# Rotary key in two products per k tile, and the residual gates' sums as split products placed inside the output projection

## The reference, cut to what matters

```python
h  = modulate(rmsnorm(x), sh1, sc1)        # 512 x 1024
hc = modulate(rmsnorm(ctx), csh1, csc1)    # 256 x 1024
p, pc = h @ w_in, hc @ w_in[:, :KR_END]    # columns: kv latent 256 | rotary key 32 | q latent 384 | conv | gates
k_rope = concat(pc[:, 256:288], rope2d(p[:, 256:288], ang))   # one 32 wide key for all 8 heads
q = rmsnorm(q latent) @ w_uq;  k_nope, v = rmsnorm(kv latent) @ w_ukv
o = softmax((q_nope k_nope' + q_rope k_rope') * scale) v
y = sigmoid(g_attn) * (o @ w_attn_out) + sigmoid(g_conv) * (conv branch @ w_conv_out)
x = x + g1 * (y @ w_o)                     # g1, g2: 1024 wide rows, from silu(c) @ w_ada + b_ada
x = x + g2 * conv_ffn(modulate(rmsnorm(x), sh2, sc2))
return rmsnorm(x) * final_g
```

## Time and profile before

| | |
|---|---|
| runs of the kernel | 827.55, 827.59, 828.06 us, median 827.59 |
| the profiled execution | 827.32 us, its span 825.3 us (2.0 us lie around the span) |
| mean granted TensorE clock | 0.994 of full |
| busy, share of the span | PE 98%, weight loads 81%, DVE 62%, ACT 45%, POOL 45% |
| matmuls | 3937 |
| moved by DMA | 97.8 MB, 119 GB/s |

### The profile page before, as it was taken

The page is one execution under the profiler, slowest core; times in us unless marked ns, Lnnn a source line. Parts: engine busy times, 40 slices in busy tenths (PEclk is TensorE's granted clock), DMA queues, the critical chain, the costliest instruction groups (busy, mean ns, idle before and its releaser), DMA issues.

```text
span 825.3 us, 11436 instructions
## 1 busy us (share of the span) xinstructions
PE 805.4 (98%) x3937; PEld 671.3 (81%) x3937; DVE 511.8 (62%) x649; ACT 371.9 (45%) x592; POOL 368.6 (45%) x193
## 2 busy tenths in 40 slices
PE   4999999999999999999999999999999999999997
PEld 3778888888888888888788988888888888888885
DVE  5877589688888388777205575455555556535535
ACT  7656575566666323223225654443344433221223
POOL 5325593535543445554534064444444442544430
PEclk9899999999999999999999999999999999999999
DMA  9742251111110887786263043332333321332212
GB/s 309 252 141 61 69 125 30 50 30 48 36 42 28 262 275 253 224 241 198 98 234 90 13 126 104 102 101 85 93 102 102 101 86 68 102 124 91 93 51 102
DMA packets 120289, 97.82 MB, mean 119 GB/s; under 512 B 13660, under 2 KB 106105, under 8 KB 120249
## 3 DMA queue, kind: packets, MB, share of 16 engines
q1 hardware_dynamic: 120137, 97.26, 38.5%
q10 hardware_dynamic: 112, 0.04, 0.0%
HBM read 95.17 MB, written 2.10 MB: 118 GB/s over the span
## 4 chain that ended last, share of the span: by engine, by line
PE 95%; DVE 2%; ACT 2%; DMA 1%; issue 0%; SPq 0%; DVEq 0%; ACTq 0%
PE ps L428 26%; PE ps L430 26%; PE ps L429 26%; PE ps L1762 8%; PE ps L1871 3%; PE ps L1860 2%; PE ps L1617 1%; DMA xt<-x_dram 1%; ACT work L749 1%; PE ps L1964 0%; PE ps L1908 0%; PE ps L1657 0%; PE ps L1916 0%; ACT parts L791 0%; DVE vs L1280 0%
## 5 line engine op out<-in xcount | busy, mean ns | idle before, releaser
L345 POOL TENSOR_TENSOR wlo<-raw,whi 128x1024 fp32r<-128x1024 f32 (+4 forms) x125 | 280.0, 2249 | 354.6 <-ACT whi L337 354.5
L428 PE MATMUL ps<-hhi,whi 128*128 128x512 f32 (+1 forms) x520 | 196.0, 377 | 0.2 <-DVE hlo L1476 0.2
L430 PE MATMUL ps<-hhi,wlo 128*128 128x512 f32 (+1 forms) x520 | 195.7, 376 | 0.0
L429 PE MATMUL ps<-hlo,whi 128*128 128x512 f32 (+1 forms) x520 | 195.5, 376 | 0.0
L337 ACT ACTIVATE whi<-raw 128x1024 fp32r<-128x1024 f32 (+4 forms) x125 | 118.3, 957 | 138.9 <-PE ps L430 48.8
L428 PEld LDWEIGHTS ps<-hhi,whi 128*128 128x128 f32 x520 | 97.8, 188 | 18.3 <-DVE hlo L1476 0.4
L430 PEld LDWEIGHTS ps<-hhi,wlo 128*128 128x128 f32 x520 | 97.8, 188 | 18.0
L429 PEld LDWEIGHTS ps<-hlo,whi 128*128 128x128 f32 x520 | 97.9, 188 | 17.7
L1502 DVE TENSOR_TENSOR raw<-raw,gbc 128x1024 f32<-128x1024 f32 x22 | 50.4, 2295 | 43.9 <-DMA raw<-w_down_dram 43.9
L1510 DVE SCALAR_TENSOR_TENSOR work<-ps,prm,work 128x511 f32<-128x511 f32 x44 | 33.0, 749 | 71.2 <-ACT work L1051 70.3
L1406 DVE SCALAR_TENSOR_TENSOR adacc<-ada,cvec,adacc 128x1024 f32<-128x1024 f32 x28 | 63.8, 2318 | 14.9 <-DMA ada<-w_ada_dram 14.9
(11 more groups left out here) (288 smaller groups left out, 1509.5 us busy)
## 6 DMA issues: line engine op xcount, KB each, us to landing
raw<-w_up_dram SPq DMA_DIRECT2D x88, 256.0 KB, 3.1
ada<-w_ada_dram SPq DMA_DIRECT2D x32, 512.0 KB, 6.1
raw<-w_in_dram SPq DMA_DIRECT2D x56, 256.0 KB, 4.4
raw<-w_down_dram SPq DMA_DIRECT2D x44, 256.0 KB, 2.8
adaraw<-w_ada_dram SPq DMA_DIRECT2D x32, 256.0 KB, 5.4
raw<-w_o_dram SPq DMA_DIRECT2D x16, 256.0 KB, 3.1
xt<-x_dram SPq DMA_DIRECT2D x4, 512.0 KB, 7.5
raw<-w_attn_out_dram SPq DMA_DIRECT2D x8, 256.0 KB, 2.9
```

What stands on the lines that cost most here:

```text
L345: ins = (engine or nc.gpsimd).tensor_tensor(out=l, in0=r, in1=h.bitcast(F32), op=ALU.subtract)
L428: pe.matmul(o, l[0], r[0], start=start, stop=False)
L429: pe.matmul(o, l[0], r[1], start=False, stop=False)
L430: return pe.matmul(o, l[1], r[0], start=False, stop=stop)
```

## The change

**The rotary key.** `key_hi` writes only the 64 key columns (32 plain, 32 swapped) of each k tile into the upper half of `whi` and then copies them, already rounded, into the upper half of `wlo`; `key_lo` zeroes the lower half of `whi` and puts the low parts into the lower half of `wlo`. `key_pair` makes two matmuls per k tile: `wlo` x hi, which gives lo x hi in rows 0 to 63 and hi x hi in rows 64 to 127, and `whi` x lo, which adds hi x lo in rows 64 to 127. The two halves have to be added: ACT copies rows 0 to 63 of banks 3 and 0 to partitions 64 to 127, behind a wait for `w_used` of `U_KR + 1`, before the squares of the kv latent; DVE adds. The key's operations for the latent tokens (`rotary_key`, four of them) move behind the reciprocals of head 1; the context's addition stays ahead of head 0. The first rotary product, which stood ahead of the sum of squares, goes.

**The gates.** ACT and DVE split the two rows into `hhi` and `hlo` (no longer read by then) in the last turn of the merge; ACT also writes ones as fp32r. `gate_rows` makes 2 x 4 fp32r matmuls into banks 4 to 7. The output projection starts with t = 0, 1 of k = 0 to 3 (48 matmuls), then the gates' sums, then t = 0, 1 of k = 4, then t = 2, 3 of k = 0 to 4, which now count `w_used`. SP's wait ahead of the residual load is for the DVE's splits and `cols2_ps` instead of the gates' sums.

```diff
-            if isinstance(u, int) and U_KR <= u < U_KR + 2:
-                return headed_raw(slot, DT // 2), headed(whi, slot, DT // 2), headed(wlo, slot, DT // 2)
...
+        def key_tiles(t, slot):
+
+            return t[:, slot, 0:DT // 2 * P].rearrange("p (k n) -> p k n", n=P)
+
+        def key_parts(v, at):
+
+            r = v[:, :, at + ROPE:at + 2 * ROPE].rearrange("p g (a h j) -> p g a h j", a=2, h=2)
+            return [v[:, :, at:at + ROPE], r[:, :, :, 0, :], r[:, :, :, 1, :]]
+
+        def key_hi(act, u, slot):
+
+            arrived(act, u, slot)
+            wait(act, w_used, u - SLOTS + 1)
+            for r, h in zip(headed_raw(slot, DT // 2), key_parts(key_tiles(whi, slot), NOPE)):
+                if h.shape[-1] == ROPE:
+                    r = r[:, :, NOPE:QK]
+                ins = nc.scalar.activation(h, r, ACT.Copy)
+            ins.then_inc(w_hi, 1)
+            act.wait_ge(w_hi, u + 1)
+            nc.scalar.activation(key_tiles(wlo, slot)[:, :, NOPE:P], key_tiles(whi, slot)[:, :, NOPE:P], ACT.Copy).then_inc(s("kr_hi"), 1)
+
+        def key_lo(pool, u, slot):
+
+            wait(pool, w_used, u - SLOTS + 1)
+            nc.gpsimd.memset(key_tiles(whi, slot)[:, :, 0:NOPE].bitcast(F32), 0.0).then_inc(s("chl_zero"), 1)
+            pool.wait_ge(w_hi, u + 1)
+            pool.wait_ge(s("chl_zero"), u - U_KR + 2)
+            for r, h, l in zip(headed_raw(slot, DT // 2), key_parts(key_tiles(whi, slot), NOPE), key_parts(key_tiles(wlo, slot), 0)):
+                if h.shape[-1] == ROPE:
+                    r = r[:, :, NOPE:QK]
+                ins = nc.gpsimd.tensor_tensor(out=l, in0=r, in1=h.bitcast(F32), op=ALU.subtract)
+            ins.then_inc(w_lo, 1)
+
...
+        kr_ctx = cx0[:, 0:C]
...
+        gate_hi, gate_lo = hhi[:, 0:4, :], hlo[:, 0:4, :]
+        ones_r = hhi[:, 4, 0:P]
+
+        def gate_value(n):
+
+            return adacc[:, 3 * n * D:(3 * n + 1) * D].rearrange("p (a n) -> p a n", n=512)
...
                 if k == 6:
-                    sp.wait_ge(s("gbc_ps"), 4)
+                    sp.wait_ge(s("ada2_used"), 4 * DT + 2)
+                    sp.wait_ge(s("cols2_ps"), 1)
...
-            for u in range(U_KR, U_UQ[2]):
+            for u in range(U_KR, U_KR + 2):
+                key_lo(pool, u, u % SLOTS)
+            for u in range(U_KR + 2, U_UQ[2]):
...
             for u in (U_KR, U_KR + 1):
-                split_hi(act, u, u % SLOTS)
+                key_hi(act, u, u % SLOTS)
...
             for u in (*U_UQ[0:2], U_CX0):
                 split_hi(act, u, u % SLOTS)
+            used(act, U_KR + 1)
+            nc.scalar.activation(krot2[NOPE:P, :], ps[0:NOPE, 3, :], ACT.Copy).then_inc(s("kr_hi"), 1)
+            nc.scalar.activation(kr_ctx[NOPE:P, :], ps[0:NOPE, 0, 0:C], ACT.Copy).then_inc(s("kr_hi"), 1)
             for m in range(KVT):
                 act.wait_ge(s("lat_ps"), QT + KVT + m + 1)
...
                     else:
+                        if d == DT - 1:
+                            act.wait_ge(s("ada2_used"), 4 * DT)
+                            for g in range(2):
+                                nc.scalar.activation(gate_hi[:, 2 * g:2 * g + 2, :], gate_value(g), ACT.Copy).then_inc(s("g_sig"), 1)
+                            nc.scalar.activation(ones_r, ones[:], ACT.Copy).then_inc(s("g_sig"), 1)
                         act.wait_ge(s("m_sum"), d + 1)
                         nc.scalar.activation(mhi[:, d, :], work[:, w + 2, :], ACT.Copy).then_inc(s("m_hi"), 1)
...
-            dve.wait_ge(s("kr_ps"), 1)
-            dve.wait_ge(s("tab_loaded"), 16)
-            kr, tmp = krot[NOPE:QK, :], krot2[NOPE:QK, :]
-            kr_ps, kr_ctx = ps[:, 3, :], ps[:, 0, 0:C]
-            nc.vector.tensor_tensor(out=kr_ps[NOPE:QK, :], in0=kr_ps[NOPE:QK, :], in1=tab[NOPE:QK, :], op=ALU.mult).then_inc(s("kr"), 1)
             dve.wait_ge(s("p_sq"), QT + 2)
             nc.vector.tensor_tensor(out=sqk[0], in0=sqk[0], in1=sqk[1], op=ALU.add).then_inc(s("k_ssq"), 1)
+            kr, low = krot[NOPE:QK, :], krot2[NOPE:P, :]
+            dve.wait_ge(s("q_sum"), QT - 1)
             used(dve, U_KR + 1)
-            nc.vector.tensor_tensor(out=tmp, in0=kr_ps[QK:P, :], in1=tab[QK:P, :], op=ALU.mult).then_inc(s("kr"), 1)
-            nc.vector.tensor_copy(kr[:, T:K], kr_ctx[NOPE:QK, :]).then_inc(s("kr"), 1)
-            dve.wait_ge(s("kr"), 3)
-            nc.vector.tensor_tensor(out=kr[:, 0:T], in0=kr_ps[NOPE:QK, :], in1=tmp, op=ALU.add).then_inc(s("kr"), 1)
+            dve.wait_ge(s("kr_hi"), 4)
+            nc.vector.tensor_tensor(out=kr[:, T:K], in0=ps[NOPE:QK, 0, 0:C], in1=kr_ctx[NOPE:QK, :], op=ALU.add).then_inc(s("kr"), 1)
+
+            def rotary_key():
+
+                dve.wait_ge(s("tab_loaded"), 16)
+                nc.vector.tensor_tensor(out=ps[NOPE:P, 3, :], in0=ps[NOPE:P, 3, :], in1=low, op=ALU.add).then_inc(s("kr"), 1)
+                dve.wait_ge(s("kr"), 2)
+                nc.vector.tensor_tensor(out=krot2[QK:P, :], in0=ps[QK:P, 3, :], in1=tab[QK:P, :], op=ALU.mult).then_inc(s("kr"), 1)
+                nc.vector.tensor_tensor(out=ps[NOPE:QK, 3, :], in0=ps[NOPE:QK, 3, :], in1=tab[NOPE:QK, :], op=ALU.mult).then_inc(s("kr"), 1)
+                dve.wait_ge(s("kr"), 4)
+                nc.vector.tensor_tensor(out=kr[:, 0:T], in0=ps[NOPE:QK, 3, :], in1=krot2[QK:P, :], op=ALU.add).then_inc(s("kr"), 1)
...
                     dve.wait_ge(s("k_rms"), 1)
                     nc.vector.reciprocal(k_inv, k_rms).then_inc(s("k_rinv"), 1)
+                    rotary_key()
...
-                    nc.vector.tensor_tensor(out=g, in0=ps[:, n, :], in1=g, op=ALU.add).then_inc(s("gbc_sum"), 1)
+                    nc.vector.tensor_tensor(out=g, in0=ps[:, 4 + n, :], in1=g, op=ALU.add).then_inc(s("gbc_sum"), 1)
...
                 if d == DT - 1:
+                    for g in range(2):
+                        dve.wait_ge(s("g_sig"), 2 * DT + g + 1)
+                        nc.vector.tensor_tensor(out=gate_lo[:, 2 * g:2 * g + 2, :], in0=gate_value(g),
+                                                in1=gate_hi[:, 2 * g:2 * g + 2, :].bitcast(F32), op=ALU.subtract).then_inc(s("ada2_used"), 1)
                     norm2_mods()
...
+            def key_pair(o, slot, k, hi, lo):
+
+                at = slice(k % 4 * P, (k % 4 + 1) * P)
+                pe.matmul(o, wlo[:, slot, at], hi[:, k, :], start=k == 0, stop=False)
+                return pe.matmul(o, whi[:, slot, at], lo[:, k, :], start=False, stop=k == DT - 1)
+
             pe.wait_ge(s("mods1"), 2 * DT)
             for n in range(2):
                 u = U_KR + n
                 unit(u)
-                last = project(pe, ps[:, 3, :], u % SLOTS, hhi[:, 4 * n:4 * n + 4, :], hlo[:, 4 * n:4 * n + 4, :], kt=DT // 2,
-                               start=n == 0, stop=n == 1)
-            last.then_inc(s("kr_ps"), 1)
+                pe.wait_ge(s("kr_hi"), n + 1)
+                for k in range(4 * n, 4 * n + 4):
+                    key_pair(ps[:, 3, :], u % SLOTS, k, hhi, hlo)
...
-                last = mm3(pe, ps[:, 0, 0:C], (tile_of(whi, u % SLOTS, k % 4), tile_of(wlo, u % SLOTS, k % 4)),
-                           (chi[:, k, :], clo[:, k, :]), k == 0, k == DT - 1)
+                last = key_pair(ps[:, 0, 0:C], u % SLOTS, k, chi, clo)
...
                 if h == 2:
-                    pe.wait_ge(s("kr"), 3)
+                    pe.wait_ge(s("kr"), 1)
...
-                pe.wait_ge(s("m_prod"), 2 * DT - 2)
-                for n, at in enumerate((0, 512, 3 * D, 3 * D + 512)):
-                    pe.matmul(ps[:, n, :], ones[:], adacc[:, at:at + 512], start=True, stop=True).then_inc(s("gbc_ps"), 1)
+                pe.wait_ge(s("m_prod"), 2 * DT)
+                pe.wait_ge(s("mods2"), 1)
+                pe.wait_ge(s("g_sig"), 2 * DT + 3)
+                pe.wait_ge(s("ada2_used"), 4 * DT + 2)
+                for n in range(4):
+                    pe.matmul(ps[:, 4 + n, :], ones_r, gate_hi[:, n, :], start=True, stop=False)
+                    pe.matmul(ps[:, 4 + n, :], ones_r, gate_lo[:, n, :], start=False, stop=True).then_inc(s("gbc_ps"), 1)
...
-            gate_rows()
...
+            pe.wait_ge(s("m_prod"), 2 * DT - 2)
             for k in range(5):
+                if k == 4:
+                    gate_rows()
                 unit(U_O + k)
                 pe.wait_ge(s("m_lo"), k + 1)
-                for t in (2, 3, 0, 1):
-                    if k == 0 and t == 2:
-                        pe.wait_ge(s("mods2"), 1)
-                        pe.wait_ge(s("m_prod"), 2 * DT)
-                    if k == 0 and t < 2:
-                        pe.wait_ge(s("gbc_sum"), 2 * t + 2)
+                for t in range(2):
+                    for n in range(2):
+                        out_rows(k, t, n)
+            for k in range(5):
+                for t in range(2, TT):
+                    if k == 0:
+                        pe.wait_ge(s("gbc_sum"), 2 * t - 2)
                     for n in range(2):
```

(23 more changed lines are left out.)

## The result

The changed kernel takes 830.05 us (median of 7 runs, 829.74 to 831.83), the kernel before 827.59 in the same comparison: ratio 1.0034, 95% interval 1.0024 to 1.0044, so 2.5 us slower. The forecast was 826.5 and a range that ended at 828.5. The profiled execution took 829.74 us, its span is 827.8 and its mean granted clock 0.995; for the kernel before these were 827.32, 825.3 and 0.994. So the mean clock of this one execution shows nothing of what follows. The other six runs of the changed kernel have 0.991 four times (829.83 to 830.32 us) and 0.987 twice (831.54 and 831.83 us), while 58 of the 59 runs of the kernel before that were taken beside the experiments have 0.992 or more.

A forecast was written before the change was run, and what follows sets the result against it. TensorE was taken as the bound, with 95% of the chain of waits. 827.32 + 0.51 - 1.57 = 826.26 us, plus 0.27 for the median of the runs, gave 826.5 us; range 825.4 to 828.5.

The forecast's parts named there:

- Part A: Rotary key: 2.76 us of matmuls removed from TensorE, all spent in waits; 0.51 us later at the first sum of squares.
- two waits: TensorE waits for DVE's first `cqlo` before the context, then for ACT's kv latent copies before the first sum of squares.
- `key_hi` itself: ACT's copies of the key's high parts: 0.94 us after the change against 0.72, so 0.22 us more.
- second stall: TensorE idle for 2.26 us before the first sum of squares, released by ACT's copies of the kv latent.
- ACT's added copies: Two new copies in front of the kv latent's squares, 64x512 and 64x256: 0.50 and 0.29 us.
- rival 4: The load of `U_CX0` lands late, delaying the sums of squares; 829.5 us at 3 us late; chance 0.04.
- Part B: Gates: eight fp32r matmuls, 1.87 us, replace four float32 sums and the change back, 3.44 us: -1.57 us.
- DVE's two subtractions: Gates: two 128x1024 operations ahead of the last products, 1.21 to 3.40 us each, ending between 401.1 and 405.5.
- The rotary key's operations: DVE gains four operations behind head 1, 2.9 us, covered by its 3.11 us idle before head 3.
- moved waits of SP: SP's new wait ends at 403, ahead of the preceding unit's need at 410, so the residual's load doesn't move.
- rival 3: New stalls of 1.0 and 2.26 us lower TensorE's clock once, costing about 1.9 us: 828.4 us; chance 0.10.
- first stall: TensorE idle about 1 us before the first context matmul, released by DVE's `cqlo`.

The follow-up runs named there:

- fill: The changed kernel plus six extra matmuls, result overwritten, in front of head 0's query product, where TensorE stalls the second time: 826.66 us.
- fill_first: The changed kernel plus four extra key products that fill the first stall and leave the second: 830.82 us, ratio 1.0031.
- a_alone: The kernel before with only the rotary key's change, the gates as before: 832.26 us, ratio 1.005.
- mended: The changed kernel; ACT copies the kv latent out before squaring, key's copies last; TensorE's context key products moved two k tiles behind the latents: 824.76 us.
- mended_fill: mended plus six extra matmuls in front of head 0's query product: 824.81 us, ratio 0.9964.
- stall_only: The kernel before plus three copies on ACT ahead of its copies of the kv latent, nothing of the change: 829.02 us, ratio 1.0025.
- copies_late: The changed kernel with ACT's two new copies moved behind its copies of the kv latent: median 826.35 us, ratio 0.9992, in two groups.

## Why the prediction was wrong

**What held.** Part A's two waits, their releasers and its sign held; its size only roughly. The forecast was +0.51. From the key's first product to the first sum of squares TensorE took 89.37 - 71.98 = 17.39 us before and 90.37 - 72.70 = 17.67 after: +0.28. The terms, with 0.72 us for the later start: the context started 0.21 us later than worked out (77.57 against 76.64 + 0.72). `key_hi` itself cost 0.24 and not 0.22, but TensorE started 0.26 behind the end of the first `cqlo` (76.57 + 0.74) and not 0.05. The context took 0.10 longer than 7.54. From start to start the second stall is therefore 90.37 - 85.21 - 3.44 = 1.72 us instead of 2.26. ACT's added copies cost 0.88 us instead of 0.79. What made the sum smaller is the load of `U_CX0`, the term of rival 4: from its issue to ACT's copy it took 85.34 - 81.03 = 4.31 us, against 84.97 - 80.13 = 4.84 before. In three more profiles with the same order on ACT it took 4.58 (`fill`), 4.59 (`fill_first`) and 5.15 (`a_alone`), and part A comes to +0.70 in `fill` (whose added matmuls stand in the wait and don't move ACT's copies) and to +1.20 in `a_alone`. So 0.51 lies inside a scatter of nearly a microsecond that mostly this load makes: the chain was right, and how near its size came is luck.

Part B: -1.57 forecast, -1.59 measured. DVE's two subtractions took 3.71 us and ended at 404.58 + 3.71 = 408.29, 0.48 behind the end of the merge, inside the bounds (from 2.6 ahead of it to 1.8 behind); `U_O + 3` came at 412.20 + 2.40 = 414.60, wanted at 416.2. The rotary key's operations were covered, as were the moved waits of SP.

**What failed is the clock: the sum had nothing for it, and rival 3 had the wrong chance and price.** I gave rival 3 0.10; it is what happened in this kernel. All 7 runs of the changed kernel lie above 829.7, where the forecast was 826.5; with the measured 3.27 on top it would have been 829.8, against a median of 830.05. For the profiled execution the terms give 827.32 + 0.72 + 0.28 + 3.27 - 0.15 - 1.59 = 829.85 us; it took 829.74. My reason against it was that 11 us of packed matmuls lie between the stalls. That looked at the wrong side. The second stall stands directly ahead of the stretch in which matmuls alternate with float32 sums of one column, and the clock fell there, behind the wait, in the first of these wide matmuls. `fill` takes most of that stall away and is 3.4 us faster. The price of 1.9 us came from nine matmuls early in the trace; here the low clock lasted for nearly 7 us and cost 3.27. Two of the seven runs stand another 1.7 us above the others. The two profiles with 13.51 instead of 11.96 show such a step of 1.55, and those two runs have the lowest mean clocks, 0.987 against 0.991; so a longer fall is the likely reason, though neither was profiled. With 1.9 us even the right rival gave 828.4, so the range was too low by its own case.

The Trainium skill (TensorE: Matmul & The Clock Gate, "HAM oscillation") ties such a fall to waits longer than any here; by it alone none of these stalls would do it. The trace differs: behind 1.05 and 1.56 us the clock fell here, and behind 0.32 us in `mended`. Its next section ("A second HAM failure mode: psum-queue depth-cycling") tells of a kernel whose clock went up and down because short idle times between groups of matmuls came often. In `mended` the idle time is short too, but it is a single one; `mended_fill`, without it, kept its clock.

**What stays open.** Idle time in front of the small sums, or among them as in `mended`, can make the clock fall: `mended_fill` against `mended` and `fill` against the changed kernel show it. That the small sums behind it matter is argued and not shown: behind the first stall, of 1.03 to 1.19 us in five profiles and in front of packed matmuls, the granted clock stayed 1.00 up to 90 us, but no run takes the small sums away. And the length of the stall doesn't order the cases. Behind 0.47 and 1.27 us there was no fall in the profiles of `fill` and `stall_only`, behind 0.32 and 0.50 there was one in `mended` and `copies_late`, and `copies_late` and `fill_first` go both ways from run to run. The exact moment of the idle time seems to matter beside its length; no run moves a stall of fixed length through the stretch, so this wasn't tested.

## What to carry to other kernels

Where TensorE is packed and already close to what another engine releases, as here, removing matmuls buys a stall, not time; then ask what follows the stall. If it is a stretch of small sums, a fraction of a microsecond of idle time can cost several times itself, so either move the deadline (here ACT's copies in another order: 824.1 us instead of 830.05) or leave the matmuls where they are. For a stall ahead of such sums, give the clock's fall a real chance and a price of its own (it made the interval 2.2 to 4.8 us longer here). Check it by an interval of equal work and by the granted clock in windows of 1 to 2 us. TensorE's busy share didn't show the 3.3 us, and the mean clock showed them only over several runs: the profiled execution alone had 0.995.

## What was not expected of the hardware

- The loss comes in steps. The same work took 8.69 to 8.77, 10.92, 11.93 or 11.96, and 13.51 us in twelve profiles, with the clock low for nothing, about 3, 7 and 10 us.
- One kernel can have two times: `copies_late` ran at 825.2 to 826.4 and at 828.7 to 829.6, and `fill_first` once at 825.97 beside nine runs from 829.96 on.
- Part A's size hangs on one load: the same transfer took 4.31 to 5.15 us from issue to ACT's copy in four profiles with the same order on ACT.
- Six added matmuls made a kernel 3.4 us faster (830.05 to 826.66) and cost another nothing (824.76 and 824.81).
